# Narrow fp32 matmuls of a two-block transformer kernel placed in four column ranges of the array

## What is computed

```python
sh1, sc1, g1, sh2, sc2, g2 = split(silu(c) @ ada_w + ada_b)             # latent tokens
csh1, csc1, cg1, csh2, csc2, cg2 = split(silu(c_ctx) @ ada_w + ada_b)   # context tokens
...
aff = softmax(h @ router_w); top_aff, idx = top_k(aff.T, cap)     # cap 128 latent, 32 context
hid = silu(xg @ w_gate[e]) * (xg @ w_up[e])                       # [cap, 512], 16 experts
y   = (hid @ w_down[e]) * top_aff                                 # [cap, 1024]
out = scatter_add(y, idx)
```

## Time and profile before

| | before |
|---|---|
| median of 3 runs | 5315.13 us (5310.35 to 5315.29) |
| the profiled execution | 5315.81 us |
| its span in the profile | 5313.3 us, granted PE clock 0.89 of full on average |
| PE busy | 88% of the span |
| DVE, ACT, POOL busy | 46%, 22%, 8% |
| HBM read and written | 395.93 MB and 55.57 MB |

### The profile page before, as it was taken

The page is one execution under the profiler, slowest core; times in us unless marked ns, Lnnn a source line. Parts: engine busy times, 40 slices in busy tenths (PEclk is TensorE's granted clock), DMA queues, the critical chain, the costliest instruction groups (busy, mean ns, idle before and its releaser), DMA issues. The chain is left out here.

```text
span 5313.3 us, 57703 instructions
## 1 busy us (share of the span) xinstructions
PE 4665.7 (88%) x22536; PEld 3496.7 (66%) x22536; DVE 2448.9 (46%) x3870; ACT 1171.6 (22%) x2091; POOL 442.3 (8%) x597
## 2 busy tenths in 40 slices
PE   8999799888999979988995799796777579998997
PEld 3887478673666659766874687585544257887875
DVE  1467678535000046677855100423433645555344
ACT  2223233220111122323322111202022222111232
POOL 0010000100121110000000111100011000000001
PEclk9999799878999989989996899898555589999999
DMA  6200000125655541000010786120000022112111
GB/s 241 84 20 1 16 2 1 64 107 197 239 202 211 190 149 40 5 15 4 0 72 32 313 329 243 64 80 25 5 0 0 0 72 72 48 48 74 48 58 52
DMA packets 75121, 454.40 MB, mean 86 GB/s; under 512 B 9872, under 2 KB 13600, under 8 KB 58912
## 3 DMA queue, kind: packets, MB, share of 16 engines
q1 hardware_dynamic: 61824, 404.34, 20.2%
q0 software_dynamic: 13088, 47.19, 3.4%
HBM read 395.93 MB, written 55.57 MB: 85 GB/s over the span
## 5 line engine op out<-in xcount | busy, mean ns | idle before, releaser
L2037 PEld LDWEIGHTS psum<-words,words 128*128 128x128 f32 x4096 | 512.6, 192 | 21.7 <-issue 21.7
L2037 PE MATMUL psum<-words,words 128*128 128x160 f32 (+1 forms) x4096 | 516.6, 288 | 1.4 <-DVE words L419 0.9
L1056 PEld LDWEIGHTS psum<-words 128*128 128x128 f32 x2928 | 400.4, 197 | 102.1 <-issue 84.4
L702 PE MATMUL psum<-words,words 128*128 128x512 f32 x1104 | 442.7, 401 | 25.0 <-DVE words L740 20.6
L703 PE MATMUL psum<-words,words 128*128 128x512 f32 x1104 | 438.8, 397 | 0.0
L704 PE MATMUL psum<-words,words 128*128 128x512 f32 x1104 | 438.8, 397 | 0.0
L1056 PE MATMUL psum<-words 128*128 128x128 f32 x2928 | 425.6, 283 | 1.7 <-DVE words L1178 1.6
L2048 PE MATMUL psum<-words,words 128*128 128x512 f32 (+1 forms) x768 | 354.7, 616 | 1.5 <-issue 1.5
L1139 DVE TENSOR_REDUCE words<-psum 128x1 f32<-128x512 f32 (+1 forms) x480 | 269.5, 561 | 99.6 <-PE psum L1239 42.1
L2104 DVE TENSOR_TENSOR words<-words,psum 128x160 f32<-128x160 f32 (+1 forms) x128 | 39.0, 305 | 578.9 <-ACT words L2082 578.9
L1097 ACT ACTIVATE words<-psum,words 128x1280 f32<-128x1280 f32 (+3 forms) x216 | 212.5, 984 | 389.1 <-DVE words L1147 214.2
(11 more groups left out here) (349 smaller groups left out, 7666.8 us busy)
## 6 DMA issues: line engine op xcount, KB each, us to landing
words<-in_w_gate SPq DMA_DIRECT2D x32, 2048.0 KB, 7.6
words<-in_w_up SPq DMA_DIRECT2D x32, 2048.0 KB, 12.0
words<-in_w_down SPq DMA_DIRECT2D x32, 2048.0 KB, 11.2
words<-in_ada_w SPq DMA_DIRECT2D x24, 2048.0 KB, 7.7
words<-in_w_in SPq DMA_DIRECT2D x55, 512.0 KB, 3.5
words<-in_w_up SPq DMA_DIRECT2D x44, 512.0 KB, 3.5
words<-in_w_down SPq DMA_DIRECT2D x44, 256.0 KB, 2.6
words<-in_x SPq DMA_DIRECT2D x2, 5120.0 KB, 17.6
```

Of the source, the lines that this page charges most:

```text
L702: pe.matmul(out, hi[:, j, w], S.parts[0](kt, t0, nt), start=(kt == 0), stop=False)
L1056: mm = pe.matmul(obanks[s % O][:, 0:P], values, pt[:, s % 2, t, :], start=(t == 0), stop=(t == nt - 1))
L2037: mm = pe.matmul(k.bank[m % 2][:, u * W:(u + 1) * W], ring[:, j, w0:w0 + P], xgT[:, j, kt, 0:W], start=(kt == 0), stop=(kt == KD - 1))
```

## The change

In `Modulation` the stationary operand becomes 32 columns wide (`cond4`: for each 128-row block 32 columns, of which the first two are the conditions and the rest zero). Block kt goes to output partitions 32 (kt mod 4) to 32 (kt mod 4) + 31, so that eight matmuls are spread over four column ranges, two to each. ACT copies all 128 rows instead of two. The turning matmuls contract over all 128 rows with a constant of two columns, `add4`, which has a one at rows s, 32+s, 64+s and 96+s: they turn and add the four partial sums at once. DVE makes both constants in `setup`.

In `experts` of layer 0 both context halves are made ahead of the latent ones, into one bank: the half h and the block kt go to partitions 64 h + 32 (kt mod 2). DVE copies the second partial sum out, adds the first to it, and scales, for each half. The signal `y_full` now counts three to an expert, and PE's wait for `y_dve` between the halves is gone.

```diff
@@ Modulation
-                               self.rows[0:2, j % 2, q * P:(q + 1) * P], k.ident[0:2, 0:2], start=True, stop=True)
+                               self.rows[:, j % 2, q * P:(q + 1) * P], k.add4[:, :], start=True, stop=True)
...
-                mm = pe.matmul(k.bank[self.banks[j % 2]][0:2, :], k.cond[:, 2 * kt:2 * kt + 2],
-                               self.ring[:, j, kt * 512:(kt + 1) * 512], start=(kt == 0), stop=(kt == KD - 1))
+                part = slice(32 * (kt % 4), 32 * (kt % 4) + 32)
+                mm = pe.matmul(k.bank[self.banks[j % 2]][part, :], k.cond4[:, 32 * kt:32 * kt + 32],
+                               self.ring[:, j, kt * 512:(kt + 1) * 512], start=(kt < 4), stop=(kt >= 4), skip_group_check=True)
...
-            act.activation(self.rows[0:2, j % 2, :], self.k.bank[self.banks[j % 2]][0:2, :], ACT.Copy).then_inc(self.taken, 1)
+            act.activation(self.rows[:, j % 2, :], self.k.bank[self.banks[j % 2]][:, :], ACT.Copy).then_inc(self.taken, 1)
@@ setup
-            pe.wait_ge(cond_set, 1)
+            pe.wait_ge(cond_set, 2)
...
+            link(dve.memset(k.cond4[:, :], 0.0))
...
-            dve.tensor_tensor(x[:, :], x[:, :], e[:, :], ALU.mult).then_inc(cond_set, 1)
+            per_kt = lambda v: v.rearrange("p (k s) -> p k s", k=KD)
+            dve.tensor_tensor(per_kt(k.cond4[:, :])[:, :, 0:2], per_kt(x[:, :]), per_kt(e[:, :]), ALU.mult).then_inc(cond_set, 1)
+            dve.wait_ge(ld, 48)
+            link(dve.tensor_tensor(k.add4[:, :], k.ident[:, 0:2], k.ident[:, 32:34], ALU.add))
+            link(dve.tensor_tensor(k.add4[:, :], k.add4[:, :], k.ident[:, 64:66], ALU.add))
+            dve.tensor_tensor(k.add4[:, :], k.add4[:, :], k.ident[:, 96:98], ALU.add).then_inc(cond_set, 1)
@@ experts
-    YF = 4 if with_ctx else 2
+    YF = 3 if with_ctx else 2
+    yt = k.at(o2 + 2 * SLOTS + 4 * D, D)
...
                     if with_ctx:
                         if old:
                             pe.wait_ge(y_dve, 2 * e)
-                        down(7, CAP_L, SLOTS, 0)
+
+                        for kt in range(4):
+                            for half in range(2):
+                                w0, r0 = 8192 + kt * D + half * 512, 64 * half + 32 * (kt % 2)
+                                mm = pe.matmul(k.bank[7][r0:r0 + CAP_C, :], hid[:, j, kt, CAP_L:SLOTS], ring[:, j, w0:w0 + 512],
+                                               start=(kt < 2), stop=(kt >= 2), skip_group_check=True)
+                        mm.then_inc(y_full, 1)
                     if old:
                         pe.wait_ge(y_act, 2 * e)
                     down(5, 0, CAP_L, 0)
                     down(6, 0, CAP_L, 1)
-                    if with_ctx:
-                        pe.wait_ge(y_dve, 2 * e + 1)
-                        down(7, CAP_L, SLOTS, 1)
...
+                        dve.wait_ge(y_full, YF * e + 1)
                         for h in range(2):
-                            dve.wait_ge(y_full, YF * e + (1 if h == 0 else 4))
-                            dve.tensor_scalar(yc[0:CAP_C, j, 512 * h:512 * h + 512], k.bank[7][0:CAP_C, :],
-                                              ac[0:CAP_C, sl(e)], None, ALU.mult).then_inc(y_dve, 1)
+                            cut, t = slice(512 * h, 512 * h + 512), yt[0:CAP_C, 512 * h:512 * h + 512]
+                            dve.tensor_copy(t, k.bank[7][64 * h + 32:64 * h + 64, :]).then_inc(yt_set, 1)
+                            dve.wait_ge(yt_set, 4 * e + 2 * h + 1)
+                            dve.tensor_tensor(t, k.bank[7][64 * h:64 * h + 32, :], t, ALU.add).then_inc(yt_set, 1)
+                            dve.wait_ge(yt_set, 4 * e + 2 * h + 2)
+                            dve.tensor_scalar(yc[0:CAP_C, j, cut], t, ac[0:CAP_C, sl(e)], None, ALU.mult).then_inc(y_dve, 1)
```

More of the change, by code:

```diff
@@ L92, in __init__ @@
         self.cond_e = const("cond_e", [P, 2 * KD])
+        self.cond4 = const("cond4", [P, KD * 32])
+        self.add4 = const("add4", [P, 2])
         self.mods = const("mods", [P, LAYERS * 6 * KD, 2])
@@ L1908, in experts @@
     acc = k.moe[l]
-    YF = 4 if with_ctx else 2
+    YF = 3 if with_ctx else 2
+    yt = k.at(o2 + 2 * SLOTS + 4 * D, D)
+    assert o2 + 2 * SLOTS + 5 * D <= SEL0
     lslot = [slots[:, j:j + 1].bitcast(U32) for j in range(2)]
@@ L1925, in experts @@
         g_in, gc_in = (g0, g1), (gc0, gc1)
-        t_full, x_act, x_dve, gu_full, silu, hid_in, y_full, y_act, y_dve = [sem() for _ in range(9)]
+        t_full, x_act, x_dve, gu_full, silu, hid_in, y_full, y_act, y_dve, yt_set = [sem() for _ in range(10)]
         @block.sync
```

## The result

| | before | after |
|---|---|---|
| median | 5315.21 us (5310.35 to 5320.47, 4 runs) | 5164.78 us (5159.44 to 5171.12, 4 runs) |
| profiled execution, its span | 5315.81, 5313.3 us | 5171.12, 5169.3 us |

What follows compares the result with a forecast made beforehand. PE was taken to bound the experts and setup, and to delay route. Experts 84.3, setup 35.3 and route 27.8, less 3, make 144.4 us off 5315.8: 5171.4, forecast 5171 us, range 5155 to 5203.

Steps and rivals of the forecast that it cites:

- PE alone bounds the expert stage; each us saved counts sixteen times: Experts of layer 0: PE alone sets the 35.08 us per expert; saving 5.27 us each gives 84.3 us.
- Four ranges at once, judged from L2324: L2324's 0.027 us step, a quarter of 0.110, means four fp32 streams at once; context down part 1.83 us; chance 0.62.
- two at a time: Rival, experts' context down product: only two column ranges run at once, experts gain 56.8 us, 5198 us; chance 0.13.
- no overlap: Rival: matmuls in one row range follow one another whatever their columns, PE's work stays, 5315 us; chance 0.05.
- drain at each change of range: Rival, experts and modulation: no overlap, and PE drains 0.2 us at each column-range change, 64 us, 5380 us; chance 0.03.
- Bare weight loads: Rival, experts' context part: weight loads wait for matmuls over the same rows, 1.6 us an expert, 5197 us; chance 0.05.
- Setup becomes bound by its loads: Modulation in setup: loads replace PE as bound, next stage's first load at 76.1 instead of 111.45, 35.3 us gained.
- slower loads: Rival, setup: loads run at 348 GB/s, x lands at 90.6, 20 us gained, 5186 us; chance 0.08.
- Route becomes bound by the top-k: Modulation in route: PE ends by 1250 to 1262, ahead of DVE's top-k at 1273.65; 27.8 us gained.
- DVE's additions and ACT's wider copy cost nothing: Experts: DVE's six operations, at most 4.5 us, cost nothing; setup: ACT's 128-row copy takes some 0.7 us beside PE.
- POOL's scatters move behind the down product; the gathers still land in time: Experts: context gather lands by +15.7 us, needed at +17.5, costs nothing; some 3 us more at the stage's end.
- The clock's loss stays: Experts: mean clock 0.97, 16 us lost; the transposes stay, so the loss is kept, bounds 16 us more or less.

## Why the prediction was right, point by point

- **PE alone bounds the expert stage; each us saved counts sixteen times.** Right: 81.5 us less, forecast 81.3. In its parts it was a little off both ways. An undisturbed expert saved 5.45 us, not 5.27: I put one change of operand width aside, but each costs on both its sides, the latent part taking 6.97 instead of 7.07 us and the gate and up product 17.55 instead of 17.65 us. The other way, the clock fell in nine experts instead of eight.
- **Four ranges at once, judged from L2324.** The step on which all hung. Right, and exact: 0.43 us for four records. With two ranges it is 3.56 us for the eight matmuls, with one 3.55 us for four: the rival "two at a time" fell, and with it "no overlap" and "drain at each change of range". Between a bound of 2 us and one of 84 us the nearest row decided: L2324's step of a quarter.
- **Bare weight loads.** Fell: loads for the same row range stand beside running matmuls. The Trainium skill's rule ("TensorE: Matmul & The Clock Gate", Part 3), that only different row groups allow this, isn't borne out here. Its measured 2.38 times for three column tiles in Part 3 would be 3.2 times for four, by the prediction's estimate; measured here are 7.10 to 1.85 us, 3.8 times, or 4.0 times in steps (6.86 to 1.71). What that estimate would have taken from the gain is worked out wrong in the prediction: 16 x (6.86 / 3.2 - 1.71) is 7 us, not 5.
- **Setup becomes bound by its loads.** Right in kind, off in size: 31.5 us against 35.3. The rate was as taken, 428 to 433 GB/s, and 12 groups at 4.89 us; by 75.97 us all but two packets had landed, against 75.5 forecast for the whole. What I left out is the end: two packets of 40 KB one after another, 3.0 us, and 0.9 instead of 0.6 us from the last one (79.00) to the next stage's load. In the same kernel's other profile the miss is 1.8 us instead of 3.8. Cutting the load in pieces didn't end it earlier than that. The rival "slower loads" (20 us) was far off.
- **Route becomes bound by the top-k.** Right: 28.0 us against 27.8, with PE waiting 17.6 us for DVE.
- **DVE's additions and ACT's wider copy cost nothing.** Right: DVE at 5.63 us of 29.62, and PE waited for neither in the expert stage; ACT's copy in setup takes 0.60 us beside the loads.
- **POOL's scatters move behind the down product; the gathers still land in time.** Right. PE never waited for a gather in the stage. The gather of context rows took 5.3 us to land, not 6.3. At the stage's end 3 us were put; from PE's end to the next stage's load it now takes 8.8 us (1753.7 to 1762.52), and took 5.6 before (1898.5 to 1904.1).
- **The clock's loss stays.** Right: nine falls of about 1.65 us, 15 us, against eight. I had named the transposes, and the experiment bears that out: with them divided there was no fall. That the number of falls stayed near eight is partly luck: other kernels run here have five, seven and ten.
- **The median.** 5171 was forecast for what turned out as 5164.78; the sum for the profiled execution, 5171.4, met 5171.12. Where the 6 us of the median lie no profile shows, but one execution differs from another by more: from the end of the expert stage to the end of the span, where nothing was changed, the profiled executions took 3406.8 us, 3393.2 (the same kernel again), 3387.3 (transposes in two) and 3409.2 (before). That an account of one execution meets it to 0.3 us is partly luck: setup gave 3.8 us less than forecast, and the untouched stages gave 2.9 us that nothing had forecast.

## What to carry to other kernels

A matmul with a stationary operand of 2 or of 32 columns took as long here as one of 128 columns, about 0.43 us a record of 512 moving columns. Where several are independent, or their sum can be split, give each a 32-column range of its own: four ran in the time of one, in fp32, and in both orders tried. First read which stage lets PE's time count: in a stage that PE bounds all of it came back, in two others only down to the next bound (DMA, DVE), and there half the parallelism would have done. And look at the granted clock behind a long row of small transposes: here 3.4 us of them were followed in nine of sixteen experts by a fall that cost 1.65 us, and narrow matmuls put between them took every fall away.

## What was not expected

- The order of matmuls among column ranges made no difference: 1.95 us with the two of a range in a row, 1.92 us with the ranges by turns.
- Four fp32 streams from the same 128 partitions run at the pace of one: 0.43 us for four records of 512 columns.
- The falls of the granted clock hung on 3.4 us of transposes in a row. Cut into 1.2 and 2.2 us, with 1.85 us of narrow matmuls between, nine falls became none and 15 us came back, with the same work.
- The thin end of a 5 MB load, single packets of 40 KB and 1.5 us one after another, differs between two executions of one kernel (last byte at 79.0 and 77.0 us). Smaller packets didn't end it earlier: in eight pieces the load moved at 415 instead of 432 GB/s, and its last byte came at 77.4 us.
